# An S5 stage's DMA queue reordered: whole modulation blocks, each ahead of the next Toeplitz round trip, and one block of row sums moved on TensorE

## The reference, cut to what matters

```python
sh1, sc1, gt1, sh2, sc2, gt2 = split(silu(c) @ w_mod + b_mod, 6)        # 2048 -> 6 * 2048
csh1, csc1, ...              = split(silu(c_ctx) @ w_mod + b_mod, 6)
h_lat = rmsnorm(x) * gain * (1 + sc1) + sh1                             # same for ctx
# S5: 128 groups of 16 channels, 64 complex states each, forward and backward
s_t   = lam_bar * s_(t-1) + b_bar @ u_t        # scan over ctx, then over x
y     = u * d + sum over both directions of real(c @ s)
z     = gelu(y); a, g = split(z @ w_glu); y = a * sigmoid(g)
x     = x + gt1 * rmsnorm(y)                   # then an MLP with sh2, sc2, gt2, then layer 2
```

## Time and profile before

| | |
|---|---|
| runs of the kernel before | 3569.63, 3572.54, 3575.3 us; median 3572.54 |
| the profiled execution | 3575.3 us, its span 3573.1 us |
| granted TensorE clock, mean | 0.949 (1 is the high level of 2.4 GHz, 0.5 the low one) |
| TensorE busy | 3305.6 us, 93% of the span |
| VectorE, ScalarE, GpSimd busy | 2148.5, 1386.5, 480.0 us |
| moved by DMA | 643 MB |

### The profile page before, as it was taken

How to read it: one execution, slowest core, us unless ns; L and a number is a source line. 1 busy time by engine, 2 the same in 40 slices (tenths; PEclk the granted TensorE clock), 3 DMA queues, 4 the chain that set the end, 5 groups by cost and what they waited for, 6 DMA issues and landing times.

```text
span 3573.1 us, 51912 instructions
## 1 busy us (share of the span) xinstructions
PE 3305.6 (93%) x21097; PEld 2771.7 (78%) x21097; DVE 2148.5 (60%) x1852; ACT 1386.5 (39%) x1390; POOL 480.0 (13%) x352
## 2 busy tenths in 40 slices
PE   5778789799999999787789999999999899999998
PEld 3445578688888888676578888888868788888887
DVE  7568755555656555589555555555654555555555
ACT  4446634433333333333234434433322344344333
POOL 2869900000000000097000000000000000000000
PEclk7788889899999999998799999999999999999999
DMA  9887765355555555344044555555523455555552
GB/s 283 297 292 239 253 239 188 106 167 186 187 188 188 188 188 188 106 139 160 22 167 158 183 188 183 182 196 180 192 99 129 141 188 188 188 187 185 189 182 92
DMA packets 351007, 643.12 MB, mean 180 GB/s; under 512 B 21599, under 2 KB 50359, under 8 KB 350519
## 3 DMA queue, kind: packets, MB, share of 16 engines
q1 hardware_dynamic: 350080, 641.37, 54.1%
q10 hardware_dynamic: 823, 0.29, 0.0%
HBM read 637.54 MB, written 4.06 MB: 180 GB/s over the span
## 4 chain that ended last, share of the span: by engine, by line
PE 83%; DVE 5%; DMA 3%; POOL 3%; issue 2%; ACT 1%; SPq 1%; DVEq 1%; ACTq 0%; POOLq 0%
PE acc L436 49%; PE acc L437 25%; DMA raw<-in_w_mod_dram 3%; POOL cpow L1805 2%; DVE z L912 1%; PE acc L1240 1%; DVE w_lo L758 1%; POOL ptmp L1805 1%; PE acc L1165 1%; PE acc L459 1%; PE acc L516 1%; PE acc L1257 1%; PE acc L528 1%; PE acc L1224 1%; PE acc L454 1%
## 5 line engine op out<-in xcount | busy, mean ns | idle before, releaser
L436 PE MATMUL acc<-xin,w_hi 128*128 128x512 f32 x5376 | 1916.1, 400 | 59.0 <-DVE xin L772 33.7
L758 DVE TENSOR_TENSOR w_lo<-raw,w_hi 128x2048 fp32r<-128x2048 f32 x488 | 1120.2, 2301 | 1085.2 <-ACT w_hi L612 1084.8
L437 PE MATMUL acc<-xin,w_lo 128*128 128x256 f32 x5376 | 1519.6, 283 | 0.0
L612 ACT ACTIVATE w_hi<-raw 128x2048 fp32r<-128x2048 f32 x488 | 934.3, 1917 | 1371.4 <-PE acc L437 1370.5
L436 PEld LDWEIGHTS acc<-xin,w_hi 128*128 128x128 f32 x5376 | 1017.4, 189 | 313.7 <-issue 36.5
L437 PEld LDWEIGHTS acc<-xin,w_lo 128*128 128x128 f32 x5376 | 1021.7, 190 | 0.0
L436 PE MATMUL acc<-hid,w_hi 128*128 128x512 f32 x2432 | 847.1, 393 | 0.0
L437 PE MATMUL acc<-hid,w_lo 128*128 128x256 f32 x2432 | 681.5, 280 | 0.0
L436 PEld LDWEIGHTS acc<-hid,w_hi 128*128 128x128 f32 x2432 | 455.3, 187 | 102.9
L437 PEld LDWEIGHTS acc<-hid,w_lo 128*128 128x128 f32 x2432 | 459.6, 189 | 0.0
L764 DVE TENSOR_REDUCE tmp<-acc 128x1024 f32<-128x2048 f32 x116 | 265.0, 2284 | 19.9 <-PE acc L437 19.9
(11 more groups left out here) (239 smaller groups left out, 2116.1 us busy)
## 6 DMA issues: line engine op xcount, KB each, us to landing
raw<-in_w_mod_dram SPq DMA_DIRECT2D x96, 1024.0 KB, 9.9
raw<-in_ffn_w_gate_dram SPq DMA_DIRECT2D x88, 1024.0 KB, 5.0
raw<-in_ffn_w_up_dram SPq DMA_DIRECT2D x88, 1024.0 KB, 5.0
raw<-in_ffn_w_down_dram SPq DMA_DIRECT2D x88, 1024.0 KB, 5.0
raw<-in_w_mlp_in_dram SPq DMA_DIRECT2D x64, 1024.0 KB, 5.4
raw<-in_w_mlp_out_dram SPq DMA_DIRECT2D x64, 1024.0 KB, 5.0
raw<-in_s_w_glu_dram SPq DMA_DIRECT2D x32, 1024.0 KB, 5.3
raw<-in_ab_w_in_dram SPq DMA_DIRECT2D x32, 1024.0 KB, 5.3
```

The source lines that it names most:

```text
L436: pe.matmul(bank, w_hi[:, slot, w], operand[:, kt, :], start=(kt == 0), stop=False)
L437: ins = pe.matmul(bank[:, 0:TOK], w_lo[:, slot, w], operand[:, kt, 0:TOK], start=False, stop=(kt == UK * units - 1))
L612: act.activation(w_hi[:, slot, :], raw[:, slot, :, :].rearrange("p k n -> p (k n)"), ACT.Copy).then_inc(hi_ready, 1)
L758: dve.tensor_tensor(w_lo[:, slot, :], raw[:, slot, :, :].rearrange("p k n -> p (k n)"), w_hi[:, slot, :].bitcast(F32), SUB).then_inc(lo_re ...
```

## The change

```diff
-            def ada_units(m, units=range(UK)):
-                col = BLOCK_COL[m]
-                for k in units:
+            def ada_units(m, col):
+                for k in range(UK):
...
             load_c(2)
+            ada_units(ADA[0], 2 * D)
             sp.wait_ge(xt_scaled, 2)
             load_x(2)
-            ada_units(4)
-
-            for n in range(KT):
-                m = ADA[n]
-                toeplitz(n, n % 2)
-                if n + 1 < KT:
-                    ada_units(m + 1, (0, 1))
+
+            for n in range(KT + 1):
+                if n < KT:
+                    toeplitz(n, n % 2)
                 if n + 3 < KT:
                     sp.wait_ge(c_sel, n + 3)
                     load_c(n + 3)
-                if n + 1 < KT:
-                    ada_units(m + 1, (2, 3))
-                if n + 3 < KT:
                     sp.wait_ge(xt_scaled, n + 3)
                     load_x(n + 3)
-                if 0 < n < 5:
-                    ada_units(m + 2)
+                if n + 1 < KT:
+                    ada_units(ADA[n + 1], (n + 1) * UN + 2 * D)
+                if n < 4:
+                    ada_units(MOD[2 + n // 2][n % 2], (1 - n % 2) * D + (2 + n // 2) * UN)
...
             transpose_e(0, 1)
+            mod_rows(1, 1)
 
             for k in range(-1, KT):
                 if k + 1 < KT:
                     lag_blocks(k + 1, (k + 1) % 2)
                     states(k + 1, (k + 1) % 2)
-                if k < 0:
-                    mod_rows(1, 1)
-                else:
+                if k >= 0:
                     outputs(k, k % 2)
```

More of the change, by code:

```diff
@@ L1038, in two_layer_kernel @@
         ADA = [4, 5, 7, 9, 11] + list(range(13, 24))
-        BLOCK_COL = {MOD[b][v]: (1 - v) * D + b * UN for b in range(4) for v in range(2)}
-        BLOCK_COL.update({m: 2 * D + n * UN for n, m in enumerate(ADA)})
         @block.sync
@@ L1060, in ada_units, with mod_units @@
                     sp.dma_start(raw[:, k, :, :], w_mod[:, k * UK:(k + 1) * UK, col:col + UN]).then_inc(raw_ready[k], 16)
+            def mod_units(b):
+                for v, col in enumerate((D, 0)):
+                    ada_units(MOD[b][v], col + b * UN)
             def load_xs(half):
@@ L1086, in _ @@
             load_xs(0)
-            ada_units(0)
+            ada_units(MOD[0][0], D)
             load_c(0)
@@ L1091, in _ @@
             load_xs(1)
-            ada_units(1)
-            ada_units(2)
+            ada_units(MOD[0][1], 0)
+            ada_units(MOD[1][0], D + UN)
             sp.wait_ge(c_sel, 1)
             load_c(1)
-            ada_units(3)
+            ada_units(MOD[1][1], UN)
             sp.wait_ge(xt_scaled, 1)
```

## The result

The changed kernel takes 3635.3 us (median of 4 runs, 3625.8 to 3642.9) against 3572.5 for the one before (4 runs, 3569.6 to 3575.3): ratio 1.0175, 95% interval 1.0148 to 1.0202. It is 63 us slower. The forecast was 10 us slower, with 3597 as the upper end. The sign held, and so did the ring that the forecast describes; the size was six times what I gave.

The account below looks back on a forecast made before the run. Bound by a 485 us S5 stage, alone affected, then 3088 us of TensorE products. 7.8 us late at iteration 13 plus 2.5 at the end makes 10.3; 3572.5 + 10 = 3582.5 us, range 3569 to 3597.

Parts of the forecast that it names:

- the ring: Iterations 5 to 12: `load_x`, ADA units, TensorE and `normalise_x` wait in a circle; 22.1 us a turn against 20.7.
- T(13): Start of `lag_blocks` in iteration 13: forecast at 433.6 against 425.76, 7.8 us late.
- X(5): End of `normalise_x`, which allows `load_x`, at the start of the seven turns: forecast 259.3 against 261.2.
- Opening: Before `lag_blocks(0)`: moved `mod_rows(1, 1)` makes nothing late; its start, held by `cpow(1)`, gains at most 1.4 us.
- Modulation blocks ahead of the round trip: Early iterations: block 6's unit 3 lands 9.5 us sooner; `lag_blocks` gains 3.7 us in iteration 1, all in iteration 2.
- A lap of 31.9 us: Iterations up to 4: time between modulation block landings in the new order, against 31.1 and 32.0 us; neither order wins.
- Iteration 4: Block 13 now follows Toeplitz, c and x loads; about six of the eight us of lead are lost.
- A: Landing of a modulation block's unit 3; for block 12 forecast at 228.2 against 236.35.
- much slower: Rival: the clock falls at every wait in turns and laps; +20 to +25 us, 3595; chance 0.12.
- The end: Iterations after 12: block ADA[15] loses its head start and outputs(15) waits longer for `tw`; adds 2.5 us.
- Near zero: Rival: turns stay at 20.7 to 20.9 us, sum 0 to +3, 3573 to 3576; chance 0.20.
- faster: Rival: the 8 us lead at iteration 4 is kept; -8 to -9 us, 3564; chance 0.13.

Follow-up runs that it names:

- the edit alone: Kernel before with only TensorE's reordering, `mod_rows(1, 1)` ahead of `lag_blocks(0)`: 3575.6 us, ratio 1.0009.
- without the ring: Changed kernel with `load_x(n+3)` and its wait moved behind the four ADA units: 3590.0 us, ratio 1.0044.
- the fillers: Changed kernel with 12 zero-adding matmuls ahead of unit 0 and 4 ahead of unit 1 in iterations 2 to 12: 3601.7 us, ratio 1.0087.
- no x ahead: Changed kernel with the x loads behind the ADA units but the wait for `xt_scaled` left ahead: 3620.2 us, ratio 1.0125.
- together: Changed kernel, x loads behind, wait left ahead, plus 8 zero-adding matmuls ahead of unit 0 and 4 ahead of unit 1: 3596.9 us, ratio 1.0056.

## Why the prediction was wrong in size, point by point

T(13) was forecast 7.8 us late and came 64.7 late. Of the 57 us between, 14.3 are there at X(5) (273.6 for 259.3), from the laps and iteration 4. The other 43 came in the ring, at 5.3 us a turn over eight turns; there lies the step that failed, the low clock taken as 0.4 us a turn.

*What bounds the kernel; only the S5 stage changes.* Right (3084.5 and 3088.1 us behind it).

*Opening.* Right: T(0) 108.97, forecast 107.7 or later; the edit alone is worth nothing.

*Modulation blocks ahead of the round trip.* Right for the first two: T(1) 140.7 after a wait of 6.41 for `cpow` (forecast 139.4), T(2) 6.7 us early (forecast 9).

*A lap of 31.9 us.* Too short. The two laps to T(4) were 39.3 and 32.8 us, 34.5 and 33.7 without the ring, and 32.7 and 33.6 in the changed kernel with the fillers, at a clock of 0.91. I let units 2 and 3 of the modulation block land in the queue's pace. The trace shows them issued late, when `ada_rows` (2,3) of the block ahead has emptied their slots (195.93 and 197.25 for block 10, 228.54 and 229.40 for block 12), and used 5.3 to 8.5 us after that. By the laps with the fillers the step missed 1 to 2 us a lap for that, and up to 6.6 in one lap for the low clock. The lead at T(4) was -1.6, not 8.

*Iteration 4.* X(5) is 273.6, the forecast 259.3. 9.7 of the 14.3 were brought along from the laps (A = 237.9 for 228.2), 1.7 came in the wait (`ada_rows` (0,1) ends at A + 18.8, not A + 17.1), 2.9 behind it (16.9 us from there to X, not 14, at the low clock).

*The ring.* Right in every link, and wrong in its two sizes. This is the step that failed, as the prediction put it: "Bounds: nothing, or 2.0 a turn ... I take 0.4, near the first, as the stretch before the wait is busy". Term by term, forecast and measured in iteration 5: x 1.3 and 1.3; unit 0 5.2 and 6.5; unit 1 2.6 and 2.8; its matmuls 1.0 and 1.9; to the end of `normalise_x` 11.6 and 15.0. With the 0.4 I had added that is 22.1 and 27.5. The clock's share, 0.9 + 3.4 = 4.3 us, was twice my upper bound. I had bounded it by unit 1 and the transposes next to it. But the low clock lasts through the output transposes (3.62 for 1.97 us), `transpose_e` (1.95 for 1.07) and `ada_rows` (2.68 for 1.92), so the second half of `transpose_e` is late, and ScalarE, which waited 0.33 us there in iterations 5 and later before, waits 2.60 for it. A rise of TensorE's time came onto the path where before ScalarE's `modulate_u` covered it.

The reason I gave for taking 0.4 was false too. The stretch before the wait for unit 1 is not busy: TensorE waited twice in a turn, 3.9 and 1.3 us, not once 1.7. In iteration 5 it stood idle from the end of outputs(5) at 277.52, so unit 0 at the 5.2 I took would still have left a wait of 2.6. And the two `lag_blocks` that I read the clock from do not carry a rule: after as long a wait as at 301.80, the one of iteration 9 in the kernel before ran at the high clock:

```profile
343.87 1.08 PE L1224 MATMUL acc<-cpow,bd 128*32 128x128 f32 x32 [2.66 <-POOL cpow L1805]
```

The row of 14.9 us in iteration 4, which I had before me and set down to that iteration, is what a turn is with the low clock.

The other term that was too small is the landing. Unit 1 is used 9.0 us after the end of the wait as a mean with no x ahead, where I had 5.2 + 2.6 = 7.8 from the opening. Why the units come later here than in the opening was not tried; x ahead of them is not the reason. The experiments bear the split out: of the 6.6 us a turn, the clock (3.5 alone) and x ahead of the units (2.0 alone, with some clock in it) make 4.9 together, and 1.7 is the bare ring over the 20.8 of before, where I had 1.0.

By the Trainium skill, TensorE: Matmul & The Clock Gate, section "HAM oscillation — how this bites in real kernels", a loop whose matmuls wait for a load each time round falls back to the low clock each time. The trace agrees (0.75 over 192 us, and 0.93 where the waits were filled); I had this as the rival "much slower" with 2 us a turn and a chance of 0.12.

*The page weighed.* By the Trainium skill, DMA: Bandwidth & Descriptors, section "Anatomy of one DMA — SWDGE (gpsimd) path", a unit takes 4.4 us to land, an estimate from that page's fit. From issue to use it was 5.05 to 6.6 in iterations 5 to 12 with no x ahead, and 5.3 to 6.5 with x ahead. All are above the page, as the rows said.

*The end.* Wrong: +2.5 forecast, -1.2 measured from T(14) (+65.1) to outputs(15) (+63.9). Turns of 27 us give SP the time to be ahead again by T(13): block ADA[15] was issued 6.7 us before T(14), earlier than before. The longer wait for `tw` at outputs(15) did not come: TensorE waited 0.20 us there, for VectorE.

*Rivals.* "Near zero" and "faster" did not come: the links of the ring have no slack between them. "Much slower" was the right kind, and too small by more than half.

## What to carry to other kernels

In a queue that issues in order, ask of each wait not only what is late behind it, but whether what is behind it is needed to end it, one iteration on: then the latencies of load, TensorE and ScalarE add up to a turn, and anything that slows one of them comes through in full. Price such a ring with TensorE's work at the low clock as the upper bound, all that it does in the turn and not only what stands next to the wait: here the ring itself made the waits. A round trip that a queue stands in is room for loads whose slots are free.

## What was not expected of the hardware

More work made the kernel faster: 16 matmuls that add zero, in each of 11 iterations took 34 us off (3635.3 to 3601.7), and what went with it was the granted clock from 300 to 400, 0.75 to 0.93. And two loads of 128 KB issued just ahead of a 1 MB unit were hardly felt beyond their own issue: the second unit was used 9.0 us after the end of the wait without them and 10.4 with them, of which 1.3 or more is their issue.
